# Ranking the tokens for the first expert: each pair of tiles compared once, the other side from column sums on TensorE

## What is computed

```python
def expert_choice_moe(x, w_router, w_gate_up, w_down):
    cap = CAPACITY_FACTOR * S // N_EXPERTS            # 128 tokens for each of 16 experts
    aff = jax.nn.softmax((x @ w_router).astype(jnp.float32), axis=-1)
    gates, idx = lax.top_k(jnp.swapaxes(aff, 1, 2), cap)
    xs = x[bi, idx]
    g, u = jnp.split(jnp.einsum('becd,edf->becf', xs, w_gate_up), 2, axis=-1)
    out = jnp.einsum('becf,efd->becd', jax.nn.silu(g) * u, w_down) * gates[..., None].astype(x.dtype)
    return jnp.zeros_like(x).at[bi, idx].add(out)
```

## Time and profile before

| what | us |
|---|---|
| median of 3 runs | 3791.79 (3790.16 to 3795.48) |
| profiled execution, its own time | 3789.95 |
| its span, first to last instruction | 3788.2 |
| PE busy in it | 3679.2 |
| DVE busy in it | 2225.6 |
| mean granted clock of the PE | 0.994 |

### The profile page before, as it was taken

The page is one execution under the profiler, slowest core; times in us unless marked ns, Lnnn a source line. Parts: engine busy times, 40 slices in busy tenths (PEclk is TensorE's granted clock), DMA queues, the critical chain, the costliest instruction groups (busy, mean ns, idle before and its releaser), DMA issues. The chain is left out here.

```text
span 3788.2 us, 63983 instructions
## 1 busy us (share of the span) xinstructions
PE 3679.2 (97%) x26734; PEld 1976.0 (52%) x26734; DVE 2225.6 (59%) x3869; ACT 1109.6 (29%) x2363; POOL 572.3 (15%) x709
## 2 busy tenths in 40 slices
PE   8999999999999999999999999998999999999998
PEld 5565756767586745545554433434444454343333
DVE  2234334666666645356667656664577788665664
ACT  2343313344353401046630111113343431111113
POOL 3332002011010022100001111110132201111110
PEclk9999999999999999999999999999999999999999
DMA  5101111000101052210069999996211259999996
GB/s 115 29 29 42 29 29 47 18 13 20 29 4 46 5 184 62 45 34 18 17 236 338 349 333 345 348 327 243 63 45 38 96 212 347 341 348 335 346 337 226
DMA packets 267326, 574.31 MB, mean 152 GB/s; under 512 B 49264, under 2 KB 123920, under 8 KB 267040
## 3 DMA queue, kind: packets, MB, share of 16 engines
q1 hardware_dynamic: 251776, 520.93, 38.9%
q0 software_dynamic: 9504, 34.61, 4.0%
q10 hardware_dynamic: 5760, 14.68, 1.0%
HBM read 521.93 MB, written 48.23 MB: 151 GB/s over the span
## 5 line engine op out<-in xcount | busy, mean ns | idle before, releaser
L4461 PE MATMUL bank<-ring,m_hidden_T 128*128 128x512 f32 x1024 | 449.4, 595 | 1.5 <-ACT m_hidden_T L4661 1.5
L4461 PEld LDWEIGHTS bank<-ring,m_hidden_T 128*128 128x128 f32 x1024 | 191.3, 190 | 232.6 <-issue 228.2
L4475 PE MATMUL bank<-ring,m_chosen 128*64 128x512 f32 x832 | 192.1, 604 | 4.0 <-POOL m_chosen L5041 4.0
L4475 PE MATMUL bank<-X,m_chosen 128*64 128x512 f32 x832 | 187.3, 592 | 0.0
L4881 DVE TENSOR_TENSOR m_junk<-bank,m_junk 128x512 f32<-128x512 f32 x26 | 18.0, 692 | 267.8 <-PE bank L4475 267.8
L4461 PE MATMUL bank<-ring,m_picked_T 128*128 128x512 f32 x384 | 167.9, 593 | 4.4 <-ACT m_picked_T L4643 2.4
L1683 PE MATMUL bank<-hnT,first_block 128*128 128x320 f32 (+3 forms) x512 | 167.7, 478 | 0.7 <-PEq L104 0.7
L4656 ACT ACTIVATE m_hidden<-m_junk 128x512 f32<-128x512 f32 x26 | 16.4, 632 | 447.6 <-DVE m_junk L4895 447.6
L4475 PEld LDWEIGHTS bank<-ring,m_chosen 128*64 128x64 f32 x832 | 58.2, 138 | 130.3 <-issue 124.6
L1683 PEld LDWEIGHTS bank<-hnT,first_block 128*128 128x128 f32 x512 | 94.5, 190 | 54.4 <-issue 11.7
L4858 DVE TENSOR_TENSOR X<-ring 128x1024 f32<-128x1024 f32 x104 | 122.5, 1221 | 0.0
(11 more groups left out here) (683 smaller groups left out, 7691.9 us busy)
## 6 DMA issues: line engine op xcount, KB each, us to landing
ring<-in_moe_w_gate_up SPq DMA_DIRECT2D x90, 2048.0 KB, 9.6
ring<-in_moe_w_down SPq DMA_DIRECT2D x256, 512.0 KB, 4.9
ring<-in_moe_w_gate_up SPq DMA_DIRECT2D x96, 512.0 KB, 9.6
m_second_ring<-in_moe_w_gate_up SPq DMA_DIRECT2D x14, 2048.0 KB, 13.6
first_block<-in_w_in SPq DMA_DIRECT2D x23, 512.0 KB, 3.9
w_block<-in_w_in SPq DMA_DIRECT2D x19, 512.0 KB, 4.2
mix<-X SPq DMA_DIRECT2D x16, 512.0 KB, 2.6
ring<-y_rows SPq DMA_DIRECT2D x16, 512.0 KB, 8.4
```

The lines of the kernel that those rows point to most:

```text
L4461: m = pe.matmul(banks[j][:, :], lhsT[:, (i % 8) * P:(i % 8 + 1) * P], ring[:, i, j, :], start=i % 8 == 0, stop=i % 8 == KD - 1)
L4475: m = pe.matmul(bank[tok[half], :], tokens_(j), weights(j)[:, 512 * half:512 * half + 512], start=j == 0, stop=j == 3)
```

## The change

For expert 0 alone, each pair of tiles is compared once. The comparison of tile t with the tiles before it (`is_ge`) is kept in a tile of its own, `ahead_of[t]`, in place of `junk`: entry (p, 128 i + j) is one where token j of tile i has an affinity not below that of token p of tile t. Its sum over p, taken by a matmul with a column of `ones`, is 128 less the number of tokens of tile t that come ahead of token j of tile i. The matmul for (i, t) has the 128x128 block of `ahead_of[t]` as its weights and moves one column; the sums of tile t land in bank 5 (bank 4 for t = 7), one column for each i. ACT copies them, negated, into slot 4 + t of the tiles i. The constant 128 (7 - i) is put into slot 4 of tile i by POOL ahead of the loop. The slots are added as before.

The sixteen comparisons of the last two kinds go, 28 matmuls, 7 copies on ACT and 7 memsets on POOL come, per layer. The matmuls for t = 1 to 4 stand in round k = 8 of the PE's loop, those for 5 and 6 in round 9, both in place of the eight `ones` matmuls there; those for 7 stand behind the turns for expert 1. Of the sixteen `ones` matmuls before the listing five are left, behind a wait for six of the ACT copies. Before each t the PE waits until the DVE has counted `before_done(t)` comparisons. `choose_vector` for expert 0 waits for all seven ACT copies, and the DVE's loop for all memsets.

```diff
-        counted, first_counts = st.sem("counted"), sum((t > 0) + (t > 4) + 2 + t % 4 for t in range(NT)) + 4
+        counted, first_counts = st.sem("counted"), sum((t > 0) + (t > 4) + 2 for t in range(NT))
+        before_done = lambda t: sum((x > 0) + (x > 4) + 2 for x in range(t)) + (t > 0) + (t > 4)
+        ahead_of = {1: xs[:, 896:1024], 2: xs[:, 640:896], 3: ys[:, 512:896], 4: ys[:, 0:512], 5: xs[:, 0:640],
+                    6: hs[:, 0:768], 7: hid[:, 0:896]}
+        behind = lambda t: ps[4 if t == NT - 1 else 5][:, 256 + NT * t:256 + NT * t + t]
+        added, subtracted = st.sem("counts_added"), st.sem("counts_subtracted")
...
+        def add_counts_tensor(pe, t):
+            pe.wait_ge(counted.sem, before_done(t))
+            for i in range(t):
+                m = pe.matmul(behind(t)[:, i:i + 1], ahead_of[t][:, P * i:P * i + P], c["ones"][:, 0:1])
+            m.then_inc(*added.up())
...
+        ADDED_AT = {8: (1, 2, 3, 4), 9: (5, 6)}
...
-                if k >= NT:
-                    keep(8)
+                for t in ADDED_AT.get(k, ()):
+                    add_counts_tensor(pe, t)
             pe.wait_ge(aff_taken.sem, NT)
             for t in range(NT):
                 spread_tensor(pe, 1, t)
-            keep(16)
+            add_counts_tensor(pe, NT - 1)
+            pe.wait_ge(subtracted.sem, NT - 2)
+            keep(5)
             list_tensor(pe, 0, ps[4])
             keep(24)
...
+            def subtract_counts(t):
+                ac.wait_ge(added.sem, max(t, NT - 2))
+                ac.activation(counts[0][:, 0:t, 4 + t:5 + t].rearrange("p i x -> p (i x)"), behind(t), ACT.Copy,
+                              scale=-1.0).then_inc(*subtracted.up())
+
+            for t in range(1, NT):
+                subtract_counts(t)
...
+            place = junk[counted.n % 4][:, 0:n * P] if kept is None else kept[:, first * P:last * P]
...
+            if x == 0:
+                ve.wait_ge(subtracted.sem, NT - 1)
             ve.tensor_reduce(rank[:, x, :], counts[x][:, :, :], AX.X, ALU.add).then_inc(*ranked[x].up())
...
-            ve.wait_ge(zeroed.sem, FAST)
+            ve.wait_ge(zeroed.sem, FAST + NT - 1)
...
-                    for i in range(t if t < 4 else 0):
-                        count_vector(ve, 0, i, t, t + 1, ALU.is_gt, c["ones"], 4 + t)
-                    for i in range(4, t):
-                        count_vector(ve, 0, i, t, t + 1, ALU.is_gt, c["ones"], 4 + t)
-            for i in range(4):
-                count_vector(ve, 0, i, 4, NT, ALU.is_gt, c["ones"], 4 + 4)
             choose_vector(ve, 0)
...
+            for t in range(NT - 1):
+                gp.wait_ge(*zeroed.now())
+                gp.memset(counts[0][:, t, 4:5], float(P * (NT - 1 - t))).then_inc(*zeroed.up())
```

More of the change, by code:

```diff
@@ L4743, in scalar, with count_vector @@
             ac.activation(lst[:, 5:6], lst[:, 4:5], ACT.Exp, scale=-0.5).then_inc(*last_rooted.up())
-        def count_vector(ve, x, t, first, last, op, weight, slot):
+        def count_vector(ve, x, t, first, last, op, weight, slot, kept=None):
             n = last - first
@@ L4750, in count_vector @@
             row = ps[2 + first // 4][:, first % 4 * P:first % 4 * P + n * P] if x else row0[:, first * P:last * P]
-            ve.scalar_tensor_tensor(junk[counted.n % 4][:, 0:n * P].rearrange("p (k j) -> p k j", j=P),
+            place = junk[counted.n % 4][:, 0:n * P] if kept is None else kept[:, first * P:last * P]
+            ve.scalar_tensor_tensor(place.rearrange("p (k j) -> p k j", j=P),
                                     row.rearrange("p (k j) -> p k j", j=P), aff[:, t, x:x + 1],
@@ L4763, in count_before_vector @@
                 if first < last:
-                    count_vector(ve, x, t, first, last, ALU.is_ge, c["ones"], i)
+                    count_vector(ve, x, t, first, last, ALU.is_ge, c["ones"], i, None if x else ahead_of[t])
         def count_behind_vector(ve, x, t):
```

## The result

The changed kernel takes 3797.85 us (median), the kernel before in the same comparison 3791.31: the ratio is 1.002, 95% interval 1.0014 to 1.0026. It is slower by 6.5 us; the forecast was faster by 4. The profiled execution takes 3796.54 us, its span is 3794.8.

A forecast was written before the change was run, and what follows sets the result against it. The prediction took the routing path up to the gathered rows' turn as the bound, once per layer: 3.1 us gained, about 2.0 left after the clock, 4.0 in all, so 3787.8 from 3791.79 us; range 3783.8 to 3794.2.

The forecast's parts named there:

- What bounds the kernel: PE busy 3679.2 of 3788.2 us; whatever comes earlier at the gathered rows' turn comes earlier at the end, once per layer.
- The DVE's part: Routing in each expert layer: with comparisons gone, the DVE finishes counting at 1949.2 instead of 1954.2, 5.0 us earlier.
- Price of the sums: The 28 new PE matmuls per layer take 0.214 us each, like the listing of expert 1; lower bound 0.12.
- Without the clock: Counting only the work of the engines, with no change of clock: 3.1 us earlier per layer, 6.2 in all.
- ACT and POOL: Six ACT copies are hidden, the seventh adds 0.3 us; seven POOL memsets end by 1924 and cost nothing.
- Tail of the weights: The gather, issued 3.1 us earlier, meets the end of the weight loading for at most 1.7 us; taken as 0.2.
- The clock: Low stretch of 3.4 us during the sums costs 1.7 per layer; up to 1.1 returns behind the listing; net gain taken 2.0.
- the third one: Clock stays low through sums and listing, 6.8 us of the PE's arm: 3794.0 us, worst 3797.8; chance 0.20.
- Signs named in advance: DVE's last comparison near 1949.2, then 1.8 us idle; pace 0.21 or 0.43; routing to turn 40 to 42 us.

The follow-up runs named there:

- late slabs: Changed kernel with each sum moving 128 columns, and the last 4 of expert 0's 24 slabs issued only when the gather has landed: 3784.43 us, ratio 0.998.
- the four versions with 128 columns: Changed kernel, every sum moving 128 columns: alone (0.9991), with sums reordered on the PE (0.9985), with late slabs (0.998), with both (0.9981).
- without the sums: Changed kernel without sums and their copies, `ones` matmuls as before (8, 8, 16), expert 0 given tokens 0 to 127: 3784.25 us, ratio 0.9988.
- with 128 columns: Changed kernel with each of the 28 sums moving 128 columns of ones in place of one, nothing else altered: 3785.05 us, ratio 0.9991.
- the idle PE: Kernel before without the 32 matmuls on `ones` ahead of the listing, so the PE idles there: 3794.88 us, ratio 1.0007.
- a PE at one column: Kernel before with the 32 matmuls on `ones` ahead of the listing moving one column instead of 128: 3801.88 us, ratio 1.0034.

## Why the prediction was wrong

- **What bounds the kernel**: right in direction, not in full. The turns of the gathered rows came 8.3 us later in all, the end 6.6 us later in the profiled executions; with late slabs 8.5 us earlier at the turns gave a ratio of 0.998, 7.6 us. Part of a shift is lost behind the second turn: from there to the last instruction it is 677.3 us before, 676.0 in the changed kernel, and 678.6 to 679.2 in the four versions with 128 columns. What takes it is not shown.
- **The DVE's part**: right. 5.0 us were forecast, 4.9 measured without the sums.
- **Price of the sums**: right. 0.214 us were forecast, and measured 0.22 to 0.23 at full clock and 0.43 at half. Without the clock 3.1 us earlier were forecast, 3.0 measured in both layers with 128 columns.
- **ACT and POOL**: right. The seventh copy takes 0.18 us, and the seven memsets end at 1924.48, 2.4 us ahead of the DVE's first operation in the loop (1926.87).
- **Tail of the weights**: undersized. I took 0.2 us; the gather lands 1.1 and 0.8 us later (5.6 and 5.2 against 4.5 and 4.4). It took back nearly all of the 1.1 us that I had expected to win behind the listing when the clock is high there: with 128 columns the gathered rows are turned 3.05 and 3.54 us earlier, with tokens 3.1 and 3.3 earlier.
- **The clock**: the step that failed. The forecast was one low stretch "as long as the present one, 3.4 us", which costs 1.7 and gives back 1.1. It came at the place forecast (1948.0) and for the reason forecast, and lasted 17 and 20 us. The error was to carry the length of the present stretch over. In the kernel before the low stretch is met by 24 matmuls of 128 columns on end, and the clock is back 3.3 and 2.7 us after their start. In the changed kernel it is met by more one-column sums, the eight turns for expert 1, five matmuls on `ones` (2.3 us) and a listing of 17 columns, through all of which the clock stayed at 0.50; it came back 4.3 and 3.8 us into the 24 matmuls. (With the idle PE it took 6.0 and 5.7 us of them.) The length depends on what runs in it, and I had held it constant. Against the 3.1 us won, the low clock cost 6.4 us in the first layer and 8.5 in the second, where 1.7 had been set down: gathered rows at 39.49 and 41.02 against 33.05 and 32.57 with the 128 columns.
- **Rivals**: the third one, slower because the clock stays low, is what happened, with 0.20 of the chance; its mechanism was right, its size was not. It counted 6.8 us of low clock on the PE's arm and 6.1 us of cost a layer at worst, against 17 and 20 us of low clock and 6.4 and 8.5 us of cost. That its worst time, 3797.8, meets the median is luck: it put too little on the clock, and took for granted that every us reaches the end. The range did not reach to it. The prediction also took 7.6 us as the least that can be told from no change; the interval told 6.5.
- **Signs named in advance**: the DVE's last comparison ends at 1950.46, which is 1949.3 when counted from the first affinity turn as before (1949.2 was said). The DVE idle with an ACT copy as its releaser came (5.26 us where 1.8 was said), and a pace of 0.43 at low clock too. Routing to turn took 45.2 us and 46.7 where 40 to 42 was said, and the 24 matmuls on `ones`, which were to end before the gather lands, ran up to the turn at 1968.28, while the gather, issued at 1962.12, took 4.4 us.
- **The page of the Trainium skill** that I weighed (TensorE: Matmul & The Clock Gate, Part 4: PE-mode transpose), by which transposes don't count as work for the clock: by it the stretch would have been longer than I took, and it was. But that does not bear the Trainium skill out: no run here separates the eight turns for expert 1 from the sums around them, and with the 128 columns the same turns ran at 1.00. The trace of the first stage speaks against that statement more plainly than I had read it. From 13.36 to 18.04 us the PE ran nothing but transposes; the clock was at 0.50 from about 14.5 us, and it came back before the first other matmul (the two stretches give length, busy us of the PE, granted clock, DMA share, GB/s):

```profile
13.36 2.97 PE L269 MATMUL bank<-ident,x_tile 128*128 128x128 f32 x16 [1.30 <-DVE x_tile L244]
16.49 1.71 PE L269 MATMUL bank<-ident,x_tile 128*128 128x128 f32 x8 [0.17 <-DVE x_tile L244]
18.04 0.73 PE L259 MATMUL bank<-hnT,first_block 128*128 128x336 f32 x2
```

```profile
17.50:17.75 0.25, 0.25 (x3) 0.50 0.00 0
17.75:18.00 0.25, 0.25 (x4) 0.90 0.00 0
```

## What to carry to other kernels

Work moved to the PE because it is idle there is not free. In matmuls that load 128 columns of weights and move one the granted clock went to half, and what stood behind them in the queue ran at half speed too, until the 24 dense matmuls behind them had run for some 4 us. Where the moved operand is narrow and the weights are not, widening it costs nothing as long as the weight load sets the pace (0.22 us for 1 as for 128 columns here), and it kept the clock: the one edit is worth some 11 us of 3798 (ratios 1.002 and 0.9991). When estimating a low stretch, look at what the PE does in it and up to the next dense run, and not at how long the last one was.

## What the runs showed of the hardware

- An f32 sum stands as two passes: 0.23 us with one column and 0.22 with 128 at a granted clock of 1.00, and 0.43 with one column at 0.50. The PE was shown as busy for 17.00 of 17.00 us at 0.50 in the changed kernel, and for 11.00 of 11.00 at 1.00 with 128 columns; the busy share in the profile did not tell the two apart.
- Since columns do not set the pace of a sum, its 0.43 against 0.23 us says that the weight load slows with the clock. The 24 matmuls on `ones` take 7.6 and 7.4 us in the changed kernel, where the clock is low in their first part, and 5.6 with the clock at 1.00.
- A PE with gaps of 2.3, 2.1 and 3.9 us lost the clock as well (17 us low), and cost 3 us a layer less than a PE at one column, because nothing stood in its queue.
- Transposes alone were enough for the clock to come back in the first stage (0.50 until 17.75 us, 1.00 from 18.0).
- The gather's landing went from 4.5 us to 5.6 and 6.1 as it was issued earlier, while the weights were still being loaded, and to 4.4 when 4 of 24 slabs were held back for it.
